# Block 2 of a two-block transformer on one core: five of the fifteen tiles of the mixer's input projection are moved between the units of its attention

## The reference, cut to what matters

```python
def second_block(x, ...):
    for l in range(DEPTH):                      # DEPTH = 2
        x = x + 0.5 * swiglu(rmsnorm_2(x, ffn1_norm[l]), ...)
        x = x + hybrid_mixing(rmsnorm_2(x, mix_norm[l]), ...)
        x = x + 0.5 * swiglu(rmsnorm_2(x, ffn2_norm[l]), ...)
    return rmsnorm_2(x, final_norm)

def hybrid_mixing(h, w_in, ...):
    z = h @ w_in                                # 1024 -> 1830 columns
    ya = mla_mixer(z[..., 0:256], z[..., 256:384], z[..., 384:416], ...)   # 6 latent heads of 96
    yb = pool_mixer(z[..., 416:672], pool_w, pool_scale)
    yc = fox_mixer(z[..., 672:1824], z[..., 1824:1830], fox_b_f)           # 6 heads of 64, forget gates
    return jnp.concatenate([ya, yb, yc], axis=-1) @ w_out
```

## Time and profile before

| what | value |
| --- | --- |
| median of three executions | 3524.66 us (3521.1 to 3525.96) |
| the profiled execution: its time, its span | 3524.67 us, 3522.9 us |
| PE busy, PE weight load busy | 3410.5 us (97%), 2804.5 us (80%) |
| DVE, ACT, POOL busy | 1836.8, 1200.4, 369.0 us |
| mixer of layer 0: first z chunk to last value product | 1936.5 to 2135.1 us |
| mixer of layer 1: the same | 2902.6 to 3103.5 us |

### The profile page before, as it was taken

How to read it: one execution, slowest core, us unless ns; L and a number is a source line. 1 busy time by engine, 2 the same in 40 slices (tenths; PEclk the granted TensorE clock), 3 DMA queues, 4 the chain that set the end, 5 groups by cost and what they waited for, 6 DMA issues and landing times.

```text
span 3522.9 us, 47185 instructions
## 1 busy us (share of the span) xinstructions
PE 3410.5 (97%) x17172; PEld 2804.5 (80%) x17172; DVE 1836.8 (52%) x2785; ACT 1200.4 (34%) x1886; POOL 369.0 (10%) x415
## 2 busy tenths in 40 slices
PE   9989999999998999999999989999999999899999
PEld 5867888888877788888888667888888886678887
DVE  5766866455357444454345665434543455654343
ACT  4354222122146332333232364323332323643232
POOL 0013200000202200020001132000200011320001
PEclk9989999999999999999999989999999999999999
DMA  6300343333220133333333302333333333023332
GB/s 220 118 29 25 96 137 106 117 130 125 61 72 24 49 95 96 96 95 95 97 99 102 83 25 60 97 99 95 90 101 96 95 96 83 25 61 98 98 95 90
DMA packets 551251, 314.75 MB, mean 89 GB/s; under 512 B 31102, under 2 KB 524888, under 8 KB 551128
## 3 DMA queue, kind: packets, MB, share of 16 engines
q1 hardware_dynamic: 550608, 312.99, 29.9%
q10 hardware_dynamic: 520, 0.13, 0.0%
HBM read 310.98 MB, written 2.10 MB: 89 GB/s over the span
## 4 chain that ended last, share of the span: by engine, by line
PE 87%; DVE 6%; ACT 4%; issue 2%; POOL 1%; DMA 0%; SPq 0%; DVEq 0%; ACTq 0%; POOLq 0%
PE ps L819 26%; PE ps L821 26%; PE ps L820 26%; PE ps L1338 2%; PE ps L1366 1%; DVE nmax L2269 1%; PE ps L974 1%; DVE scr L1956 1%; ACT scr L1730 1%; PE ps L1304 1%; ACT w_hi_sb L1398 1%; DVE hl_lat L1944 0%; PE ps L1138 0%; DVE x_ctx L1784 0%; PE ps L1244 0%
## 5 line engine op out<-in xcount | busy, mean ns | idle before, releaser
L1779 DVE TENSOR_TENSOR w_lo_sb<-w_raw,w_hi_sb 128x1024 fp32r<-128x1024 f32 (+1 forms) x460 | 588.5, 1280 | 1236.3 <-ACT w_hi_sb L1398 1234.7
L1398 ACT ACTIVATE w_hi_sb<-w_raw 128x1024 fp32r<-128x1024 f32 (+1 forms) x460 | 506.3, 1101 | 1382.2 <-PE ps L821 1351.4
L819 PE MATMUL ps<-hh_lat,w_lo_sb 128*128 128x512 f32 x1808 | 720.1, 398 | 6.0 <-DVE w_lo_sb L1779 1.9
L820 PE MATMUL ps<-hl_lat,w_hi_sb 128*128 128x512 f32 x1808 | 706.0, 391 | 0.0
L821 PE MATMUL ps<-hh_lat,w_hi_sb 128*128 128x512 f32 x1808 | 705.6, 390 | 0.0
L819 PEld LDWEIGHTS ps<-hh_lat,w_lo_sb 128*128 128x128 f32 x1808 | 341.2, 189 | 84.6 <-issue 6.7
L820 PEld LDWEIGHTS ps<-hl_lat,w_hi_sb 128*128 128x128 f32 x1808 | 340.9, 189 | 74.9 <-issue 6.3
L821 PEld LDWEIGHTS ps<-hh_lat,w_hi_sb 128*128 128x128 f32 x1808 | 340.6, 188 | 72.2
L819 PE MATMUL ps<-h2h,w_lo_sb 128*128 128x512 f32 x704 | 275.2, 391 | 1.9 <-DVE z L2240 1.5
L820 PE MATMUL ps<-h2l,w_hi_sb 128*128 128x512 f32 x704 | 274.0, 389 | 0.0
L819 PE MATMUL ps<-m2h,w_lo_sb 128*128 128x512 f32 x704 | 273.9, 389 | 0.0
(11 more groups left out here) (361 smaller groups left out, 5359.7 us busy)
## 6 DMA issues: line engine op xcount, KB each, us to landing
w_raw<-in_ffn_w_gu SPq DMA_DIRECT2D x176, 512.0 KB, 3.8
w_raw<-in_w_ff SPq DMA_DIRECT2D x128, 512.0 KB, 4.0
w_raw<-in_ffn_w_down SPq DMA_DIRECT2D x64, 704.0 KB, 4.5
z<-in_w_mod SPq DMA_DIRECT2D x64, 512.0 KB, 5.1
w_raw<-in_w_in SPq DMA_DIRECT2D x56, 512.0 KB, 3.8
w_raw<-in_w_out SPq DMA_DIRECT2D x32, 512.0 KB, 3.9
scr<-in_w_mod SPq DMA_DIRECT2D x16, 512.0 KB, 5.1
scr<-in_w_mod SPq DMA_DIRECT2D x2, 2048.0 KB, 14.5
```

What stands on the lines that cost most here:

```text
L819: nc.tensor.matmul(dst, wl, hi[:, k, 0:n], start=(k == 0), stop=False)
L820: nc.tensor.matmul(dst, wh, lo[:, k, 0:n], start=False, stop=False)
L1398: nc.scalar.activation(w_hi_sb[:, slot, 0:width], w_raw[:, slot, 0:width], ACT.Copy).then_inc(S["w_hi"], 1)
L1779: nc.vector.tensor_tensor(w_lo_sb[:, slot, 0:width], w_raw[:, slot, 0:width], w_hi_sb[:, slot, 0:width].bitcast(F32), ALU.subtract).then_i ...
```

## The change

Only the first ten tiles are made in `linear_z2`. Chunks 10 to 14 are made in six pieces of four matmuls each, one piece behind the scores of each of units 0 to 29 (`PART = 6`), all into PSUM bank 0. The small work that followed chunk 9 moves into the units as well: `mla_query` 4 and 5, `mla_keys` 1 and 2, both `pooled`, the three `fox_values`, with their copies and rotations on ACT and DVE, and the running sum. They all use PSUM bank 1. Therefore the scores of units 0 to 31 (`S_WIDE = 32`) have two banks instead of four, and those of units 32 and 33 wait until tile 14 has been taken. In the first ten chunks the order of the small work changes: second mean square after chunk 3 instead of 4, queries 0 and 1 after chunk 5, keys 0 after chunk 6, `prepare2` of heads 0 and 1 at chunk 8, and the gates' Exp and Ln behind it. `prepare2` comes at units 3 and 5 of each eight instead of 1 and 3. The first two splits of `linear_r` move from units 2 to 4 to units 30 and 31. Buffers are placed elsewhere (`split2`, `att_p`, `out_home`), and `linear_r` reads the first two output tiles from there (`run_mixed`).

```diff
+        Z2_AHEAD = 10
+        PART = 6
+        S_WIDE = 32
+        def chunk_of(u):
+            return Z2_AHEAD + u // PART
+        def chunk_ends(u):
+            c = chunk_of(u) - 1
+            return c if u and u % PART == 0 and c < len(Z2_TILES) else None
+        def next_split(u):
+            c = 16 if u == S_WIDE - 1 else chunk_ends(u) and chunk_ends(u) + 1
+            return c + 1 if c else None
...
-            b = 2 * (u % 2) if st.first else u % 4
+                b = 2 + u % 2 if u < S_WIDE else u % 4
...
-            return 2 if st.first else 4
+            return 2 if st.first or u < S_WIDE else 4
...
-            at = (1, 3) if st.nq > 2 else (0, 2)
+            at = ((1, 3) if st.nq > 2 else (0, 2)) if st.first else (3, 5)
...
+                def beside_units(st, u):                                     # PE
+                    z2, mx = st.z2, st.mixer
+                    c, part = chunk_of(u), u % PART
+                    if c < len(Z2_TILES):
+                        if part == 0:
+                            pe.wait_ge(S["w_lo"], z2.chunk0 + c + 1)
+                            pe.wait_ge(S["z_taken"], z2.at("z_taken", max(c, Z2_AHEAD - 1) if c > Z2_AHEAD else Z2_AHEAD - 1))
+                        n = 3 * KD // PART
+                        mm = products(bank(0), c % 2, KD, hh_lat, hl_lat, T, part=range(part * n, (part + 1) * n))
+                        if part == PART - 1:
+                            mm.then_inc(S["chunk_done"], 1)
+                    if u == 1:
+                        pe.wait_ge(S["z_taken"], z2.at("z_taken", Z2_AHEAD))
+                        mla_keys(mx, 1)
+                    if u == 3:
+                        pe.wait_ge(S["mla_kc"], mx.at("mla_kc", 8))
+                        mla_query(mx, 4)
+                    if u in (5, 7):
+                        pe.wait_ge(S["mla_qc"], mx.at("mla_qc", 5 + (u - 5) // 2))
+                        pe.wait_ge(S["mla_qf"], mx.at("mla_qf", 5 + (u - 5) // 2))
+                        if u == 5:
+                            mla_query(mx, 5)
+                        else:
+                            mla_keys(mx, 2)
+                    if u in (9, 11):
+                        j = (u - 9) // 2
+                        if j == 0:
+                            pe.wait_ge(S["mla_kc"], mx.at("mla_kc", 12))
...
+                    if u in (13, 15, 17):
+                        j = (u - 13) // 2
+                        if j == 0:
+                            pe.wait_ge(S["pool_t"], mx.at("pool_t", 2))
+                        else:
+                            pe.wait_ge(S["fox_vc"], mx.at("fox_vc", j))
...
-                            if c == 4:
+                            if c == 3:
                                 pe.wait_ge(S["mla_sq"], mx.at("mla_sq", 3))
...
+                            if not st.first and u in (S_WIDE, S_WIDE + 1):
+                                pe.wait_ge(S["z_taken"], st.z2.at("z_taken", len(Z2_TILES)))
...
                             if u < U:
                                 scores(u)
+                                if not st.first:
+                                    beside_units(st, u)
...
+                    if u == 0:                                               # ACT
+                        query_copy(mx, 3)
+                    if u == 2:
+                        key_copies(mx, 1)
+                    if u in (4, 6):
+                        query_copy(mx, 4 + (u - 4) // 2)
+                    if u == 8:
+                        key_copies(mx, 2)
...
+                    if u in (14, 16, 18):
+                        j = (u - 14) // 2
+                        act.wait_ge(S["fox_vt"], mx.at("fox_vt", j + 1))
+                        nc.scalar.activation(zt(11 + j), bank(1), ACT.Copy).then_inc(S["fox_vc"], 1)
...
+                    c = next_split(u)
+                    if c is not None:
+                        split(st.z2.chunk0 + c, c % 2, KD, z2_width(st.z2, c))
...
+                            if c == 7:                                       # ACT, linear_z2
+                                key_copies(mx, 0)
+                            if c in (7, 8):
+                                for t in range(2 * (c - 7), 2 * (c - 7) + 2):
+                                    act.wait_ge(S["mla_v"], mx.at("mla_v", t + 1))
+                                    nc.scalar.activation(v_mla[:, t, :], bank(4 + t % 2, 384), ACT.Copy).then_inc(S["mla_vc"], 1)
+                            if c == 8:
+                                prepare2(mx, 0)
+                                prepare2(mx, 1)
...
+                    if u in (0, 1):                                          # DVE
+                        rope_query(mx, 2 + u)
+                    if u == 2:
+                        dve.wait_ge(S["fox_e"], mx.at("fox_e", 2))
+                        link(nc.vector.tensor_tensor(fox_t[0], fox_t[3], fox_t[0], ALU.subtract))
...
+                    if u in (4, 6):
+                        rope_query(mx, 4 + (u - 4) // 2)
...
+                            if not st.first:
+                                ahead_of_unit(st, u)
```

More of the change, by code:

```diff
@@ L657, in out_tile, with out_home, mixed_tile @@
             return hd // 2 if hd < MLA_H else 5 + (hd - MLA_H) // 2
+        def out_home(st, pair):
+            if not st.first and pair < 2:
+                return scr_tile(4992 + 2 * T * pair), scr_tile(5504 + 2 * T * pair)
+            m = out_tile(st, 2 * pair)
+            return HH[st.s][:, m, :], HL[st.s][:, m, :]
+        def mixed_tile(st, k):
+            if st.block2 and k < 2:
+                return out_home(st.attention, k)
+            return hh_lat[:, k, :], hl_lat[:, k, :]
         with nc.Block() as block:
@@ L811, in _, with products @@
             def _(pe):
-                def products(dst, wslot, kt, hi, lo, n, before=None):
-                    for k in range(kt):
-                        if before is not None:
+                def products(dst, wslot, kt, hi, lo, n, before=None, part=None):
+                    for i in part or range(3 * kt):
+                        k, j = divmod(i, 3)
+                        if before is not None and j == 0:
                             before(k)
@@ L929, in sums_of, with mla_query, mla_keys @@
                                 column_sums(n, b)
+                def mla_query(mx, hd):
+                    for k in range(2):
+                        mm = nc.tensor.matmul(q_bank(hd), wq_b[:, k, hd, :], zt(k), start=(k == 0), stop=(k == 1))
+                    mm.then_inc(S["mla_q"], 1)
+                def mla_keys(mx, pair):
+                    heads = wkv_b[:, 0, 2 * pair:2 * pair + 2, :].rearrange("p h f -> p (h f)")
+                    nc.tensor.matmul(k_bank(pair), heads, zt(2), start=True, stop=True).then_inc(S["mla_k"], 1)
@@ L1739, in _ @@
                                 hi_copy(HH[s2][:, 4 + g, :], zt(6 + g, s2)).then_inc(S["gm_hi"], 1)
-                            if not st.first and u == 6:
-                                for j in range(2):
-                                    act.wait_ge(S["pool_t"], st.mixer.at("pool_t", j + 1))
-                                    hi_copy(hh_lat[:, 3 + j, :], zt(3 + j)).then_inc(S["pool_hi"], 1)
                             if u < U and prepares(st, u):
@@ L1749, in _ @@
                                     prepare2(st, prepares(st, u))
[L1750 to L1751 removed]
+                            if not st.first and u < U:
+                                beside_units(st, u)
                         take_out(st, st.heads // 2 - 1)
@@ L2292, in _ @@
                                 low(HL[s2][:, 4 + g, :], zt(6 + g, s2), HH[s2][:, 4 + g, :]).then_inc(S["gm_lo"], 1)
-                            if not st.first and u == 7:
-                                for j in range(2):
-                                    dve.wait_ge(S["pool_hi"], st.mixer.at("pool_hi", j + 1))
-                                    low(hl_lat[:, 3 + j, :], zt(3 + j), hh_lat[:, 3 + j, :]).then_inc(S["pool_lo"], 1)
                             if u < U and prepares(st, u):
```

398 lines of the change are left out of this document (207 added, 191 removed).

## The result

The changed kernel takes 3563.17 us (median of four executions, 3558.16 to 3565.41), the kernel before 3522.94 (four, 3521.1 to 3525.96): ratio 1.0111, 95% interval 1.0099 to 1.0123. It is 40 us slower where 9 were forecast.

The account below looks back on a forecast made before the run. PE was taken to bound the kernel almost everywhere. Per layer, 74.4 + 1.3 + 53.7 + 39.3 + 10.6 + 24.0 = 203.3 us against 198.6, so 9.4 us more in all: 3534 us, range 3508 to 3550.

Parts of the forecast that it names:

- The sign: Whole kernel: slower, by 4.7 us a layer and 9.4 in all; chances slower 0.50, same 0.24, faster 0.26.
- Only stretches where PE is not fed can pay: Whole kernel: PE is the bound almost everywhere (97% busy), so gains can come only where it is not fed, as in the mixer.
- The two new waits: Chunks 0 to 9: PE waits 2.0 us for the third square after chunk 3, and 2.4 more for values after chunk 7.
- Units 0 to 15: Attention's first units: work 38.0 plus waits 15.7 from in-order engines, in all 53.7 us against 25.6 before.
- 38.0: PE's work in units 0 to 15, in us: two pairs, 16 pieces, queries, keys, pooled products and two groups of transposes.
- Units 16 to 31: Attention's next units: work 35.4 plus waits 3.9, in all 39.3 us against 29.6 before.
- The tile at unit 24: Units 18 and 24: no `prepare2` stands ahead of the tile, so it is taken in time.
- Units 32 to 35: Output-projection splits meet units 30 and 31, with pooled high and low parts behind: 4.6 us more, 10.6 against 6.0.
- the clock: Rival, layer 0's attention: half of 14.12 busy us at 1.2 GHz now on the path, 4 us more a layer, 3542; chance 0.14.
- waits as worked out: Likeliest case, whole kernel: the waits come at their worked-out sizes, 3527 to 3541 us; chance 0.46.
- The overlap pays: Rival, units 0 to 35: waits under 19.5 us a layer make it faster; with half the waits, 12.1, 3510 us; chance 0.26.
- No net change: Rival, chunks 0 to 9: both new waits turn out covered, 2.0 and 2.4 us a layer less, 3525 us; chance 0.14.

Follow-up runs that it names:

- experiment 9: On experiment 6, output-projection splits, pooled high and low parts and tile 13 moved into gaps where ACT or DVE waits for the other: 3498.21 us, 0.9924.
- experiment 10: Changed kernel with pieces of one product in place of four, so the last five tiles are not the projection's: 3555.82 us, 1.0092.
- experiment 2: Changed kernel with ACT squaring the third tile beside chunk 2 and copying the first values ahead of the first four key copies: 3548.2 us, 1.0068.
- experiment 5: Changed kernel with the edits of experiment 1, experiment 2 and experiment 3 together, and later transpose groups at units 16 and 18: 3516.38 us, 0.9984.
- experiment 3: Changed kernel with pooled instructions, gates, scan, rope of query 2 and rotated keys moved to chunks 7 and 8, plain key copies one unit sooner: 3543.29 us, 1.0049.
- experiment 4: Changed kernel with output-projection splits moved from units 30 and 31 to 40 and 41, pooled high and low parts to 42 to 44: 3560.1 us, 1.0097.
- experiment 8: Changed kernel with six unused filler products on PE at each of units 30 and 31: 3561.12 us, 1.0112.
- experiment 1: Changed kernel with DVE taking a finished tile out of bank 0 one unit sooner, ahead of that unit's low parts: 3555.19 us, 1.0083.
- experiment 6: On experiment 5, PE makes the piece and small product last in each unit, behind the turn and the values: 3506.81 us, 0.9954.

## Why the prediction was right and wrong, step by step

**The sign, and the bound.** Slower was right, and that the waits come from order and not from load is shown: the same work in another order is 65 us faster (experiment 9). "Only stretches where PE is not fed can pay" holds for products too: a quarter of the pieces' work gave almost the same time as all of it (experiment 10).

**Chunks 0 to 9.** The two new waits are there: 1.67 for 2.0 at the second mean square, 4.02 for 4.0 at the values; the stretch with query 3 took 77.65 for 75.7. Experiment 2 took 4.07 us of waits away and got 5.92 back. The 1.9 us that were missed go with the 3.4 us at half clock behind the wait.

**Units 0 to 15.** Forecast 53.7, measured 60.25 / 57.8. The waits came place by place: 1.45 for 2.8 at unit 2, 0.85 and 3.52 for 1.0 and 3.9 at unit 3, 2.70 for 2.6 at unit 6, 1.80 for 1.7 at 9, 2.08 for 2.0 at 12, 1.51 for 1.1 at 15. The term that failed is the work, "38.0": it measured 46.0 in layer 0. At full clock it is 40.1 (experiment 5), so 2.1 us are a size taken too small. The other 5.9 are there only together with the waits: 10.2 us at half clock, at 0.40 to 0.46 us each, are 4.1 to 4.7, and the rest I put, without an experiment for it, to what starts again behind a wait. Profiles with the same unit work narrow this. PE's own share is 42.4 us with 3.4 at half clock and 43.3 with 6.9 (the two layers of experiment 3), and 45.2 and 46.0 with 10.3 and 10.2 (the two layers of the changed kernel). That is near 0.5 us each and leads to an estimate of 41 at full clock (experiment 5 has one group of transposes less in these units), so the work was taken some 3 us too small and the clock can be nearly all of the rest. Waits and half clock fell together in these runs, so a cost of starting again is not excluded. Query 4 shows both: forecast 1.31, measured 2.45 from 2031.87 to the next scores at 2034.32, directly behind its wait.

**Units 16 to 31.** Waits 4.10 for 3.9, work 38.7 for 35.4. At full clock the work is 37.1 (experiments 3 and 4, layer 1): 1.7 of size, 1.6 of clock. The tile at unit 24 was late (1.90), where the prediction said that it is taken in time: it saw that no low part of the queries stands ahead, and overlooked the outputs' low part of unit 22 with the maximum of 23 behind it. The sum of the waits is right by luck: this 1.90 stands in the place of the 1.4 for the last tile, whose wait (1.58) comes only at unit 32 and counts in the next stretch.

**Units 32 to 35.** 13.0 for 10.6. The waits sum to 5.88, 5.4 more than before (0.51), where 4.6 more were forecast; 1.58 of them are the last tile's. That all waits of units 0 to 35 come to 24.2, the forecast's very sum, is therefore chance in part. That the two splits stood at the wrong units was right; that moving them alone would have helped is refuted (experiment 4).

**The sum.** Layer 0 is 14.5 us over. Counted up: half clock and restarts 1.9 + 5.9 + 1.6, work taken too small 2.1 + 1.7 (by the estimate of 41 us about 1 moves from the first group to the second), waits -1.5 + 0.2, units 32 to 35 2.4, and 0.2 is left.

**The step that failed is that the clock was put as a rival of the waits.** "If half of those 14.12 now lies on the path ... 4 us more a layer" had a chance of 0.14 beside 0.46 for "waits as worked out". In fact the clock's loss mostly rides on the waits: where they went it went too (the ten chunks in experiment 2 and units 0 to 15 in experiment 5, both at 1.00), and where PE waits for ACT anyway a better clock buys nothing (experiment 8). It is no strict rule: in experiment 1 units 16 to 31 of layer 0 keep their 4.1 us of waits, and the half clock in them rises from 3.4 to 10.0 us. So the likeliest case, 74.4 + 1.3 + 53.7 + 39.3 + 10.6 + 24.0, added full waits to work at full clock and had nothing for the 9.4 us of layer 0 that the runs put to half clock and restarts; its work was 3.8 too small besides. The line "or half clock for more than 17 us a layer, which would make it slower still" came true with some 30.6 us, but it was no test: the kernel before has 27.2 over the same stretches, and what differs is where they lie. The Trainium skill (TensorE: Matmul & The Clock Gate, HAM oscillation) charges a kernel that idles between bursts with half of its throttled time; the pairs of layers here give 0.39, 0.40 and 0.46 in a stretch that PE fills and experiment 2 gives 0.55, near that rule, and there is nothing in units 32 to 35. By that rule the 10.2 us of units 0 to 15 would be 5.1.

**The method.** I added PE's work and PE's waits as if they were independent. Most waits were sized rightly (that at unit 2 by half), but the sum could not tell what removing one gives: 20.7 us of work less gave 1.8 us in units 0 to 31 of layer 0 and took 1.2 more in layer 1, and 10.6 came in layer 0's units 0 to 15 from PE's order alone. The waits of 14.21 us were themselves half made by the place of the piece and the small product ahead of the turn. The prediction named the scores that queue behind query 4; it did not follow the turn behind it to ACT's copy and the next exponential.

**The rivals.** "The overlap pays" was put at less than 19.5 us of PE's waits in units 0 to 35. It was wrong for this kernel (24.2) and right as a mechanism: with 2.99 + 4.69 + 5.12 = 12.8 us (experiment 5) the ratio is 0.9984, with 4.6 (experiment 9) 0.9924. But its price was too generous: for 12.1 us of waits I had given 3510, and experiment 5 has 3516, since the work is larger than in my sum. "No net change" is refuted: both waits in chunks 0 to 9 were there.

## What to carry to other kernels

When work is put between the units of a pipeline, first ask what stands behind it on its own engine: a product that may wait belongs behind the turn that another engine needs, not ahead of it. A wait of A for B that is followed by a wait of B for A can cost both, so follow a wait through the queued work until it comes back to the engine that caused it. Then price it with the clock, which fell here with added waits (chunks 0 to 9, experiment 2) and with thinned work (experiment 10), and put jobs without a due time in the gaps where an engine waits for the other's half of the same tile.

## What the runs showed of the hardware that I had not expected

- A us at 1.2 GHz cost 0.39 to 0.55 us in a stretch that PE fills and nothing where PE waits for ACT (experiments 2, 3, 4, 6 and 8). Nearly the same amount at half clock, 27.2 us before and some 30.6 after, can be nearly free or not.
- Less work for PE lowered its clock: with a quarter of the products in each piece, units 0 to 31 of layer 0 were at half clock for 44.4 us in place of 13.6 (experiment 10).
- Two layers of one execution repeat their stretches to 0.1 us (42.76 and 42.82, 12.97 and 12.98, 24.13 and 24.12) where the clock is the same, so the other layer is a control that costs no run. The place of the half clock counts too: units 0 to 15 take 60.25 and 57.78 us at 0.92 and 0.91.
- The pieces' interleaving with `float32` products and transposes costs little: 16 units with 16 pieces and their small products take 39.0 us of PE at full clock (39.98 less 0.94 of waits, experiment 6) where the sum of the parts was 38.0, one group of transposes more in it.
